# V in one piece, turned blocks in one piece, and four PSUM banks around layer 1's attention

## The chip, the cores and the metric

The kernel runs on one core of a Trainium2 chip. The metric is the device time of one execution in microseconds (us), here the median of several runs. Profiles are of one execution each. A core has TensorE (PE; its weight loads are PEld), VectorE (DVE), ScalarE (ACT), GpSimd (POOL), SyncE (SP, which here issues nearly all DMAs), and 16 DMA engines.

## What is computed

A two-layer backbone over 1024 latent tokens and 256 context tokens, width 1024, all in fp32. Layer 0 mixes with pooling and differential attention, layer 1 with multi-head latent attention; each layer ends with a SwiGLU. The change lies in layer 1's mixer:

```python
    def keys_values(a):
        b, n, _ = a.shape
        ckv = a @ w_dkv
        c_kv = rmsnorm(ckv[..., :MLA_KV_RANK], kv_lat_g)
        k_rope = ckv[..., MLA_KV_RANK:]
        kvh = (c_kv @ w_ukv).reshape(b, n, MLA_HEADS, MLA_NOPE + MLA_V)
        k = jnp.concatenate([kvh[..., :MLA_NOPE],
                             jnp.broadcast_to(k_rope[:, :, None, :], (b, n, MLA_HEADS, MLA_ROPE))], axis=-1)
        return rmsnorm(k, k_g), kvh[..., MLA_NOPE:]
...
    o_l = sweep_query_blocks(lambda qi, kk, vv: attn_core(qi, kk, vv, scale), q_l, k_all, v_all)
    out_l = o_l.reshape(b, n, MLA_HEADS * MLA_V) @ w_out
```

There are 16 heads, with 96 values per query and key (64 and 32 rotated) and 64 per V. The last layer needs latent queries only, so scores are 1024 queries by 1280 keys per head.

## The kernel before

All products are made from a high and a low part: fp32 operands are split into `hi` (rounded) and `lo` (the rest), and a product is three matmuls, hi x hi, hi x lo and lo x hi (`products`, L163). BANK is 512 fp32 columns, a PSUM bank; T is 1280 tokens in TT = 10 tiles of 128, LAT 1024 in QT = 8 tiles.

`heads1` (L656) goes through the 10 token tiles. For a tile, PE projects the queries (3 banks, L163 with `h1_wqh`; tiles 0 to 7 only), the keys (2 banks) and V in two halves of 512 columns (banks 5 and 2). DVE and ACT norm q and k. Between these projections PE turns blocks: turned block n takes two heads and 256 tokens by four transposes (L858) into a PSUM bank, ACT takes the high part out with its gain (`high`, L893), DVE the low part (`low`, L965), and SP stores both to DRAM (`store_turn`, L743). There are 72 such blocks, eight a tile, 20 slots behind the tile's own work, so that blocks 44 to 71 come in tiles 8 and 9 and after them. Block n uses one of two banks (TB + n % 2), so PE waits for `low` of block n - 2; the high and low parts lie in a ring of OUTS = 4 buffers each, so ACT waits for the stores of block n - 4. V goes the same way without a turn: `value_high` on ACT (L926), `value_low` on DVE (L1017), and two stores a half (L750).

In DRAM, q and k lie as one row of all tokens for each head, part (high or low) and value index: (32, 96, 1024) and (32, 96, 1280). A store of a block writes 192 pieces of 1 KB, a load of a head's k reads 96 pieces of 5 KB and of q 96 of 4 KB. V lies as two tensors, high and low.

`attention1` (L1066) then goes through the 16 heads; before it there is a barrier of all engines. Per head SP loads q high, k high, q low, k low (L1116, L1118) and then V high and V low (L1123, pieces of 256 B) into one of two buffers by the head's parity. The loads of head h wait until the scores of head h - 2 are done (`st`), V's also for the last product with V of that head (`pv`). PE first makes 20 units of high x high scores (`aux`, L1154 and L1159, two banks XB) whose maxima DVE takes (`read_aux`, L1228, L1230), then the negative maximum (L1234) is turned into a row of q (L1150, L1223). For head 0 all this is ahead of the loop; for head h + 1 it is spread over key tiles 1 to 8 of head h. In the loop, per key tile, PE makes scores of the next tile (six matmuls L163), ACT takes two exponentials a half (L1296, L1297), POOL their difference (L1323), and PE multiplies with V (L1184 to L1186). At the start DVE prepares constant rows (L1268 to L1275), for which PE waits (`rows`).

Each engine works strictly in the order of its own program; waits are on semaphores.

## Time and profile before

| | us |
|---|---|
| median of 3 runs | 3428.92 |
| lowest and highest | 3427.8, 3430.4 |
| the profiled execution's own time | 3422.42 |
| its span | 3420.6 |
| PE busy | 3168.6 (93%) |
| DVE, ACT, POOL busy | 1839.0, 973.2, 1507.9 |

The span is the time from the first to the last instruction. Times in the rows count from its start. `heads1` runs from about 1785 to 1982, `attention1` from there to about 2578. An engine's busy share over the whole says little about either; windows, waits and the timeline do. A wait is put down to the last releaser that the profile shows.

### The profile page before, as it was taken

How to read it: one execution, taken by the hardware profiler on the slowest of the kernel's cores; microseconds unless marked ns; L12 is line 12 of the kernel's file. 1: busy time of each engine (PE TensorE's matmuls, PEld its weight loads, DVE VectorE, ACT ScalarE, POOL GpSimd, SP SyncE). 2: the span in 40 equal slices, each digit the busy share in tenths (PEclk: the TensorE clock that was granted, in tenths of full speed). 3: DMA queues.
4: the chain of work that ended last, by engine and by line, in shares of the span. 5: the costliest groups of instructions: out<-in, count | busy, mean ns of one | idle time of the engine just before them, and what ended most of it. 6: DMA issues, size and time to landing. Idle time of an engine off the chain costs nothing. (4 is left out here: it accounts for less than half of the span.)

```text
span 3420.6 us, 42918 instructions
## 1 busy us (share of the span) xinstructions
PE 3168.6 (93%) x15030; PEld 2599.5 (76%) x15030; DVE 1839.0 (54%) x2477; ACT 973.2 (28%) x1698; POOL 1507.9 (44%) x1157
## 2 busy tenths in 40 slices
PE   7997987799999999999889879999996999999999
PEld 6775775588888888888677657777775788888887
DVE  5584876655444444444526757777666433333333
ACT  4322664131000000000424536666661300000000
POOL 3683543543322332222522237777787533332332
PEclk9998998899999999999989979999998999999999
DMA  6466221412222222222214862332314211111111
GB/s 225 130 198 174 55 55 64 156 56 73 69 65 64 61 61 63 65 67 62 80 48 157 263 174 63 69 73 58 84 29 154 62 50 44 53 44 43 55 49 62
DMA packets 160193, 297.26 MB, mean 87 GB/s; under 512 B 53345, under 2 KB 98145, under 8 KB 159969
## 3 DMA queue, kind: packets, MB, share of 16 engines
q1 hardware_dynamic: 148576, 254.08, 25.2%
q10 hardware_dynamic: 11520, 41.95, 4.3%
q8 instruction: 54, 0.88, 0.1%
q14 instruction: 43, 0.34, 0.0%
HBM read 233.06 MB, written 62.91 MB: 87 GB/s over the span
## 5 line engine op out<-in xcount | busy, mean ns | idle before, releaser
L127 POOL TENSOR_TENSOR small<-ident 128x1 f32<-128x1 f32 x170 | 53.8, 316 | 1165.9 <-PE ps L163 663.5
L163 PE MATMUL ps<-hidden,whi 128*128 128x512 f32 (+1 forms) x1760 | 500.7, 370 | 8.6 <-POOL wlo L138 5.1
L1323 POOL TENSOR_TENSOR a_pl<-a_p,a_ph 128x512 fp32r<-128x512 f32 x320 | 430.4, 1367 | 173.6 <-ACT a_p L1297 173.2
L1989 DVE SCALAR_TENSOR_TENSOR residual<-ps,mod,residual 128x512 f32<-128x512 f32 (+1 forms) x440 | 302.6, 696 | 376.1 <-PE ps L163 376.0
L138 POOL TENSOR_TENSOR wlo<-raw,whi 128x1024 fp32r<-128x1024 f32 x170 | 440.7, 2592 | 14.2
L163 PE MATMUL ps<-mixed_hi,whi 128*128 128x512 f32 (+1 forms) x1200 | 426.5, 355 | 14.3 <-POOL wlo L138 10.4
L163 PE MATMUL ps<-mixed_lo,whi 128*128 128x512 f32 (+1 forms) x1200 | 425.3, 354 | 0.0
L163 PE MATMUL ps<-mixed_hi,wlo 128*128 128x512 f32 (+1 forms) x1200 | 424.9, 354 | 0.0
L163 PEld LDWEIGHTS ps<-hidden,whi 128*128 128x128 f32 x1760 | 320.3, 189 | 65.4 <-POOL wlo L138 5.2
L1800 ACT ACTIVATE hidden<-gated 128x512 fp32r<-128x512 f32 (+1 forms) x110 | 64.9, 590 | 999.9 <-DVE gated L1978 999.8
L1978 DVE TENSOR_TENSOR gated<-gated,ps 128x512 f32<-128x512 f32 (+1 forms) x110 | 69.8, 635 | 511.6 <-PE ps L163 495.4
L163 PE MATMUL ps<-o_hi,whi 128*128 128x512 f32 x800 | 314.1, 393 | 24.6 <-POOL wlo L138 20.6
L163 PE MATMUL ps<-hidden,wlo 128*128 128x512 f32 (+1 forms) x880 | 324.6, 369 | 0.0
L163 PE MATMUL ps<-o_hi,wlo 128*128 128x512 f32 x800 | 312.8, 391 | 0.0
L163 PE MATMUL ps<-o_lo,whi 128*128 128x512 f32 x800 | 312.7, 391 | 0.0
L163 PE MATMUL ps<-a_q,a_k 97*128 97x512 f32 x960 | 270.1, 397 | 0.8 <-DVE a_q L1223 0.8
L163 PEld LDWEIGHTS ps<-mixed_hi,whi 128*128 128x128 f32 x1200 | 227.3, 189 | 48.4 <-POOL wlo L138 11.0
L163 PEld LDWEIGHTS ps<-mixed_lo,whi 128*128 128x128 f32 x1200 | 227.4, 190 | 31.4
L163 PEld LDWEIGHTS ps<-mixed_hi,wlo 128*128 128x128 f32 x1200 | 227.1, 189 | 31.7
L1296 ACT ACTIVATE a_ph<-ps 128x512 fp32r<-128x512 f32 x320 | 192.4, 601 | 182.0 <-PE ps L163 180.8
L1228 DVE TENSOR_REDUCE a_top<-ps 128x1 f32<-128x512 f32 x256 | 176.2, 691 | 75.5 <-PE ps L1154 70.5
L163 PEld LDWEIGHTS ps<-a_q,a_k 97*128 97x128 f32 x960 | 180.5, 190 | 38.9 <-DVE a_q L1223 1.0
(293 smaller groups left out, 6079.3 us busy)
## 6 DMA issues: line engine op xcount, KB each, us to landing
raw<-in_w_ffn SPq DMA_DIRECT2D x132, 512.0 KB, 3.6
l_vraw<-in_mod_t ACTq DMA_DIRECT2D x56, 512.0 KB, 3.7
raw<-in_w_out SPq DMA_DIRECT2D x32, 512.0 KB, 3.7
a_k<-scratch_k SPq DMA_DIRECT2D x32, 480.0 KB, 6.8
f_vraw<-in_mod_t ACTq DMA_DIRECT2D x24, 512.0 KB, 4.2
a_q<-scratch_q SPq DMA_DIRECT2D x32, 384.0 KB, 5.7
a_k<-scratch_k SPq DMA_DIRECT2D x32, 320.0 KB, 7.3
a_v<-scratch_v SPq DMA_DIRECT2D x32, 320.0 KB, 5.1
```

Of the source, the lines that this page charges most:

```text
L127: e.nc.gpsimd.tensor_tensor(e.spare[:, 0:1], e.ident[:, 0:1], e.ident[:, 0:1], ALU.mult)
L138: nc.gpsimd.tensor_tensor(e.wlo[:, s, 0:n], e.raw[:, s, 0:n], e.whi[:, s, 0:n].bitcast(F32), ALU.subtract).then_inc(e.split_done, 1)
L163: last = nc.tensor.matmul(out, a, b, start=at == 0, stop=at == n - 1)
L1228: nc.vector.tensor_reduce(top[:, q:q + 1, c], e.ps[:, bank:bank + BANK], AX.X, ALU.max).then_inc(s["auxr"], 1)
L1296: nc.scalar.activation(ph[:, kk % 2, c], b, ACT.Exp).then_inc(s["exp"], 1)
L1323: nc.gpsimd.tensor_tensor(pl[:, kk % 2, c], p[:, kk % 2, c], ph[:, kk % 2, c].bitcast(F32), ALU.subtract).then_inc(s["pl"], 1)
L1800: nc.scalar.activation(hh[:, y, a:a + w], hm[:, a:a + w], ACT.Copy).then_inc(s["hi"], 1)
L1978: nc.vector.tensor_tensor(hm[:, a:a + w], sg[:, a:a + w], e.ps[:, 3 * BANK + a:3 * BANK + a + w], ALU.mult).then_inc(s["prod"], 1)
L1989: last = nc.vector.scalar_tensor_tensor(h[:, m, a:a + w], e.ps[:, o:o + w], e.mod[:, g, c:c + 1], h[:, m, a:a + w], ALU.mult, ALU.add)
```

## The change

- V is stored whole, one store a half, from `value_high` alone; the DVE step `value_low` leaves `heads1`. In `attention1` V is loaded whole (one load a head) into a new buffer, ACT copies it into the high part at key tile 4 of the head before (`value_high`), and DVE subtracts at key tile 5 (`value_low`). V's load now waits only for that subtraction two heads earlier.
- In DRAM q and k lie as (8 pairs of heads, 2 parts, 96, groups of 256 tokens, 2 heads, 256). A store of a block is 96 pieces of 2 KB; a load of q is 96 x 4 pieces of 1 KB, of k 96 x 5.
- At the start of `attention1` SP loads high q and high k of head 0 on a semaphore of their own and waits for them before it issues the rest.
- The first 20 maxima and the two rows after them go round four banks (XB and OB) instead of two; the turned blocks from n = 44 on go round four (TB and the query banks, free by then).

```diff
@@ heads1
+        vw = sb("h1_v", [128, 2, BANK], F32)
...
+        WIDE = 8 * QT - 20
+        def turn_bank(n):
+            return TB + n % 2 * BANK if n < WIDE else (TB, TB + BANK, QB, QB + BANK)[(n - WIDE) % 4]
+        def turn_before(n):
+            return max((m for m in range(n) if turn_bank(m) == turn_bank(n)), default=None)
...
                     for x, buf in enumerate((oh, ol)):
-                        to = dst[4 * u8:4 * u8 + 4, :, 256 * g:256 * g + 256].rearrange("(h x) d t -> x d h t", x=2)
-                        sp.dma_start(to[x, :, :, :], buf[:, n % OUTS, :].rearrange("p (h t) -> p h t", h=2).bitcast(F32))\
+                        sp.dma_start(dst[u8, x, :, g, :, :].rearrange("d h t -> d (h t)"), buf[:, n % OUTS, :].bitcast(F32))\
...
                 def store_v(t, half):
-                    sp.wait_ge(s["vlo"], n + 1)
-                    for x, buf in enumerate((vh, vl)):
-                        sp.dma_start(S["v1"][x, t, :, half * BANK:(half + 1) * BANK], buf[:, n % 2, :].bitcast(F32))\
-                          .then_inc(vstored[n % 2], 16)
+                    sp.wait_ge(s["vcopy"], n + 1)
+                    sp.dma_start(S["v1"][t, :, half * BANK:(half + 1) * BANK], vw[:, n % 2, :]).then_inc(vstored[n % 2], 16)
...
-                    if n >= 2:
-                        pe.wait_ge(s["lo"], n - 1)
-                    bank = TB + (n % 2) * BANK
+                    if turn_before(n) is not None:
+                        pe.wait_ge(s["lo"], turn_before(n) + 1)
+                    if n >= WIDE:
+                        pe.wait_ge(s["qs"], 2 * QT)
+                    bank = turn_bank(n)
...
-                def value_low(t, n):
-                    dve.wait_ge(s["vhi"], 2 * t + n + 1)
-                    nc.vector.scalar_tensor_tensor(vl[:, n, :], e.ps[:, VBANK[n]:VBANK[n] + BANK], rc[:, t:t + 1], vh[:, n, :].bitcast(F32),
-                                                   ALU.mult, ALU.subtract).then_inc(s["vlo"], 1)
@@ attention1, SP
-                def load(h, par, first):
+                def load(pair, par, first):
+                    h = pair * 2 + par
                     if not first:
                         sp.wait_ge(s["st"], h * 2 * KS - 2 * KS)
                     for x in range(2):
+                        at = s["early"] if first and par == 0 and x == 0 else s[f"qk{par}"]
...
+                        if at is s["early"]:
+                            sp.wait_ge(at, 32)
                     if not first:
-                        sp.wait_ge(s["pv"], h * KS - KS + 2)
-                    for x, at in ((0, 0), (1, 2 * VD1)):
-                        sp.dma_start(vs[:, par, :, at:at + VD1].bitcast(F32),
-                                     S["v1"][x, :, :, bass.ds(h * VD1, VD1)].rearrange("t p v -> p t v"))\
-                          .then_inc(s[f"v{par}"], 16)
+                        sp.wait_ge(s["vlo"], h)
+                    sp.dma_start(vw[:, par, :, :], S["v1"][:, :, bass.ds(h * VD1, VD1)].rearrange("t p v -> p t v"))\
+                      .then_inc(s[f"v{par}"], 16)
@@ attention1, PE
-                def aux(g, par, u):
+                def aux(g, par, u, first=False):
                     bank = XB + (u % 2) * BANK
+                    if first:
+                        bank = (XB, XB + BANK, OB, OB + BANK)[u % 4]
                     if u == 0:
-                        pe.wait_ge(s[f"qk{par}"], (g - par) * 32 + 64)
+                        if first:
+                            pe.wait_ge(s["early"], 32)
+                        else:
+                            pe.wait_ge(s[f"qk{par}"], (g - par) * 32 + 64)
...
-                    pe.wait_ge(s["auxr"], g * AUX + u + 1)
+                    if not first:
+                        pe.wait_ge(s["auxr"], g * AUX + u + 1)
+                    elif u >= 4:
+                        pe.wait_ge(s["auxr"], u - 1)
@@ attention1, DVE
+                    if kk == 5 and more:
+                        value_low(h + 1, 1 - par)
+                def value_low(g, par):
+                    dve.wait_ge(s["vhi"], g + 1)
+                    nc.vector.tensor_tensor(vs[:, par, :, 2 * VD1:3 * VD1], vw[:, par, :, :], vs[:, par, :, 0:VD1].bitcast(F32),
+                                            ALU.subtract).then_inc(s["vlo"], 1)
@@ attention1, ACT
+                    if kk == 4 and more:
+                        value_high(h + 1, 1 - par)
+                def value_high(g, par):
+                    act.wait_ge(s[f"v{par}"], (g - par) * 8 + 16)
+                    nc.scalar.activation(vs[:, par, :, 0:VD1], vw[:, par, :, :], ACT.Copy).then_inc(s["vhi"], 1)
@@ scratch
-            ("q1", (HEADS1 * 2, QK1, LAT), F32), ("k1", (HEADS1 * 2, QK1, T), F32),
-            ("v1", (2, TT, 128, HEADS1 * VD1), F32), ("h", (KT, 128, LAT), F32))}
+            ("q1", (HEADS1 // 2, 2, QK1, LAT // 256, 2, 256), F32), ("k1", (HEADS1 // 2, 2, QK1, T // 256, 2, 256), F32),
+            ("v1", (TT, 128, HEADS1 * VD1), F32), ("h", (KT, 128, LAT), F32))}
```

SP's order at the entry of attention stands like this before (`a_q`, `a_k`, `a_v` are head 0's and then head 1's buffers):

```order
L1116 DMA a_q<-scratch_q 96x1024
L1118 DMA a_k<-scratch_k 96x1280
L1116 DMA a_q<-scratch_q 96x1024
L1118 DMA a_k<-scratch_k 96x1280
L1123 DMA a_v<-scratch_v 128x10x64 x2
```

and like this in the changed kernel, where `a_vw` is the new buffer for whole V and `f_mfull3` is the number that the new semaphore got:

```order
L1119 DMA a_q<-scratch_q 96x4x256
L1121 DMA a_k<-scratch_k 96x5x256
L1119 DMA a_q<-scratch_q 96x4x256 [waits f_mfull3]
L1121 DMA a_k<-scratch_k 96x5x256
L1127 DMA a_vw<-scratch_v 128x10x64
```

The wait now stands between the high and the low parts, the pieces are 256 columns, and one load of V is gone.

PE's first products of head 0 (units 0 to 15 are 512 columns wide), before; `f_stored0` is what DVE's reading of a maximum raises:

```order
L1154 MATMUL ps<-a_k,a_q 128x512 [waits f_stored0,f_mfull4,f_vfull0]
L1154 MATMUL ps<-a_k,a_q 128x512 [waits f_stored0] x15
```

and changed:

```order
L1165 MATMUL ps<-a_k,a_q 128x512 [waits f_mfull3,f_vfull0]
L1165 MATMUL ps<-a_k,a_q 128x512 x3
L1165 MATMUL ps<-a_k,a_q 128x512 [waits f_stored0] x12
```

The first product waits for the new semaphore and, as before, for the constant rows (`f_vfull0`); three more follow with no wait for DVE.

DVE in the last token tile of `heads1`, before (`h_vl` is V's low part, `h_ol` a turned block's, L982 the sum of squares of k):

```order
L1017 SCALAR_TENSOR_TENSOR h_vl<-ps,heads_spare,h_vh 128x512 [waits f_xa7]
L965 SCALAR_TENSOR_TENSOR h_ol<-ps,h_kgain,h_oh 96x512 [waits f_xa5]
L982 TENSOR_REDUCE heads_spare<-heads_spare 128x16 [waits f_rot,f_root]
L965 SCALAR_TENSOR_TENSOR h_ol<-ps,h_kgain,h_oh 96x512 [waits f_xa5]
L1017 SCALAR_TENSOR_TENSOR h_vl<-ps,heads_spare,h_vh 128x512 [waits f_xa7]
L965 SCALAR_TENSOR_TENSOR h_ol<-ps,h_kgain,h_oh 96x512 [waits f_xa5] x2
```

and changed:

```order
L974 SCALAR_TENSOR_TENSOR h_ol<-ps,h_kgain,h_oh 96x512 [waits f_xa5] x2
L991 TENSOR_REDUCE heads_spare<-heads_spare 128x16 [waits f_rot,f_root]
L974 SCALAR_TENSOR_TENSOR h_ol<-ps,h_kgain,h_oh 96x512 [waits f_xa5] x3
```

Both subtractions for V are gone; the order of the rest is the same.

## Rows read from the trace of the kernel before

**Rows 1.** The page, the chain that ended last: shares of the span by engine.

```profile
PE 23%; DVE 1%; issue 0%; POOL 0%; ACT 0%; DMA 0%; DVEq 0%; SPq 0%; POOLq 0%
```

**Rows 2.** Windows: us, busy PE, PEld, DVE, ACT, POOL, granted clock, DMA share, GB/s.

```profile
1925.00:1958.00 33.00, 26.20 (x127) 18.93 (x127) 23.52 (x35) 18.38 (x30) 6.02 (x6) 0.90 0.90 280
1958.00:1982.00 24.00, 10.52 (x48) 6.42 (x48) 11.62 (x17) 8.34 (x13) 1.05 (x1) 0.64 0.89 272
```

**Rows 3.** Waits of PE, 1850 to 1925: us in total, times, longest us.

```profile
PE ps L858 <- DVE h_ol L965: 5.7, 4, 1.4
```

**Rows 4.** Waits of PE and of ACT, 1925 to 1958.

```profile
PE ps L858 <- DVE h_ol L965: 5.8, 8, 1.4
...
ACT h_oh L893 <- DMA scratch_q<-h_ol: 4.8, 4, 2.5
```

**Rows 5.** Waits of PE and of ACT, 1958 to 1982.

```profile
PE ps L858 <- DVE h_ol L965: 8.7, 10, 2.0
...
ACT h_oh L893 <- DMA scratch_k<-h_ol: 6.4, 6, 2.0
```

**Rows 6.** Timeline at the entry: start us, us, what, [idle before <- releaser].

```profile
1982.13 0.34 SPq L1116 DMA_DIRECT2D a_q<-scratch_q  x1
...
1989.11 0.49 DVE L1275 CAST a_v<-sel 128x640 fp32r<-128x640 f32 x1
...
1991.27 1.19 PE L1154 MATMUL ps<-a_k,a_q 96*128 96x512 f32 x2 [15.17 <-DMA a_k<-scratch_k]
...
1992.08 1.29 DVE L1228 TENSOR_REDUCE a_top<-ps 128x1 f32<-128x512 f32 x2 [2.48 <-PE ps L1154]
...
1993.65 1.29 DVE L1228 TENSOR_REDUCE a_top<-ps 128x1 f32<-128x512 f32 x2 [0.29 <-PE ps L1154]
...
2007.60 0.18 DVE L1234 TENSOR_REDUCE a_negmax<-a_top 128x8 fp32r<-128x24 f32 x1
...
2010.59 5.38 PE L163 MATMUL ps<-a_q,a_k 97*128 97x512 f32 x12 [0.79 <-DVE a_q L1223]
```

**Rows 7.** Windows, the loop.

```profile
2070.00:2500.00 430.00, 419.92 (x1882) 322.63 (x1880) 309.37 (x408) 279.20 (x519) 332.78 (x246) 1.00 0.31 69
```

**Rows 8.** Waits of PE, 2016 to 2500.

```profile
PE ps L1154 <- DMA a_k<-scratch_k: 3.0, 4, 1.3
```

**Rows 9.** Groups, 1785 to 1982: busy us, mean ns of one | idle before.

```profile
L1017 DVE SCALAR_TENSOR_TENSOR h_vl<-ps,heads_spare,h_vh 128x512 fp32r<-128x512 f32 x20 | 14.8, 740 | 4.2 <-ACT h_vh L926 4.1
...
L926 ACT ACTIVATE h_vh<-ps,heads_spare 128x512 fp32r<-128x512 f32 x20 | 13.6, 681 | 15.0 <-PE ps L163 15.0
```

**Rows 10.** Windows: q and k of head 0; the residual in 4 KB pieces.

```profile
1984.00:1986.00 2.00, 0.00 (x0) 0.00 (x0) 1.97 (x4) 0.00 (x0) 0.00 (x0) 0.50 1.07 305
...
2008.00:2010.00 2.00, 1.80 (x8) 1.61 (x8) 0.86 (x2) 0.00 (x0) 0.00 (x0) 0.50 1.02 408
```

**Rows 11.** Windows: q and k in the loop (4, 5 KB); V (256 B).

```profile
2048.00:2049.00 1.00, 1.00 (x6) 0.70 (x4) 0.00 (x0) 1.00 (x2) 1.00 (x2) 1.00 1.01 254
...
2052.00:2053.00 1.00, 0.34 (x2) 0.30 (x2) 0.00 (x0) 0.61 (x2) 0.80 (x2) 1.00 1.37 219
```

**Rows 12.** Timeline, the last turned blocks.

```profile
1973.49 0.68 ACT L893 ACTIVATE h_oh<-ps,h_kgain 96x512 fp32r<-96x512 f32 x1 [1.00 <-PE ps L858]
...
1975.17 0.75 DVE L965 SCALAR_TENSOR_TENSOR h_ol<-ps,h_kgain,h_oh 96x512 fp32r<-96x512 f32 x1 [0.22 <-ACT h_oh L893]
...
1976.14 0.68 ACT L893 ACTIVATE h_oh<-ps,h_kgain 96x512 fp32r<-96x512 f32 x1 [1.00 <-PE ps L858]
```

**Rows 13.** The page, DMA issues: count, KB each, median us from issue to landing.

```profile
scratch_k<-h_oh SPq DMA_DIRECT2D x40, 192.0 KB, 2.8
```

**Rows 14.** Timeline in the loop: ScalarE ahead of a key tile's first exponential.

```profile
2063.46 0.60 ACT L1296 ACTIVATE a_ph<-ps 128x512 fp32r<-128x512 f32 x1 [1.42 <-PE ps L163]
```

**Rows 15.** Timeline, a head without a wait: its load's issue, its first product.

```profile
2114.08 0.34 SPq L1116 DMA_DIRECT2D a_q<-scratch_q  x1
...
2123.08 0.44 PE L1154 MATMUL ps<-a_k,a_q 96*128 96x512 f32 x1
```

More of the change, by code:

```diff
@@ L760, in _ @@
                 for x in range(2):
-                    sp.wait_ge(vstored[x], 32 * TT)
+                    sp.wait_ge(vstored[x], 16 * TT)
             @block.gpsimd
@@ L834, in value @@
                     if n == 0 and t:
-                        pe.wait_ge(s["vlo"], 2 * t - 1)
+                        pe.wait_ge(s["vcopy"], 2 * t - 1)
                     if n == 1:
@@ L924, in value_high @@
                     if t:
-                        act.wait_ge(vstored[n], 32 * t)
-                    nc.scalar.activation(vh[:, n, :], e.ps[:, VBANK[n]:VBANK[n] + BANK], ACT.Copy, scale=rc[:, t:t + 1]).then_inc(s["vhi"], 1)
+                        act.wait_ge(vstored[n], 16 * t)
+                    nc.scalar.activation(vw[:, n, :], e.ps[:, VBANK[n]:VBANK[n] + BANK], ACT.Copy, scale=rc[:, t:t + 1]).then_inc(s["vcopy"], 1)
                 for x in range(7):
@@ L1060, in _ @@
                     low(t, 6)
-                    if t < TT:
-                        value_low(t, 1)
                     low(t, 7)
@@ L1074, in attention1 @@
         vs = sb("a1_v", [128, 2, TT, 3 * VD1], F32R)
+        vw = sb("a1_vw", [128, 2, TT, VD1], F32)
         p = sb("a1_p", [128, 2, LAT], F32)
@@ L1079, in attention1 @@
         ident = sb("a1_ident", [128, 128], F32R)
-        s = {x: sem("a1_" + x) for x in ("qk0", "qk1", "v0", "v1", "rows", "aux", "auxr", "neg", "st", "exp", "pl",
-                                         "pv", "raw", "rec", "whole", "ohi", "out", "x")}
+        s = {x: sem("a1_" + x) for x in ("early", "qk0", "qk1", "v0", "v1", "rows", "aux", "auxr", "neg", "st", "exp", "pl",
+                                         "pv", "raw", "rec", "whole", "ohi", "out", "x", "vhi", "vlo")}
         OB, XB = 4 * BANK, 6 * BANK
@@ L1115, in load @@
                     for x in range(2):
-                        sp.dma_start(qs[0:QK1, par, x, :].bitcast(F32), S["q1"][bass.ds(h * 2 + x, 1), :, :]
-                                     .rearrange("o p t -> p (o t)")).then_inc(s[f"qk{par}"], 16)
-                        sp.dma_start(ks[0:QK1, par, x, :].bitcast(F32), S["k1"][bass.ds(h * 2 + x, 1), :, :]
-                                     .rearrange("o p t -> p (o t)")).then_inc(s[f"qk{par}"], 16)
-                    if not first:
-                        sp.wait_ge(s["pv"], h * KS - KS + 2)
-                    for x, at in ((0, 0), (1, 2 * VD1)):
-                        sp.dma_start(vs[:, par, :, at:at + VD1].bitcast(F32),
-                                     S["v1"][x, :, :, bass.ds(h * VD1, VD1)].rearrange("t p v -> p t v"))\
-                          .then_inc(s[f"v{par}"], 16)
+                        at = s["early"] if first and par == 0 and x == 0 else s[f"qk{par}"]
+                        sp.dma_start(qs[0:QK1, par, x, :].rearrange("d (g t) -> d g t", t=256).bitcast(F32),
+                                     S["q1"][bass.ds(pair, 1), x, :, :, par, :].rearrange("o d g t -> d (o g) t")).then_inc(at, 16)
+                        sp.dma_start(ks[0:QK1, par, x, :].rearrange("d (g t) -> d g t", t=256).bitcast(F32),
+                                     S["k1"][bass.ds(pair, 1), x, :, :, par, :].rearrange("o d g t -> d (o g) t")).then_inc(at, 16)
+                        if at is s["early"]:
+                            sp.wait_ge(at, 32)
+                    if not first:
+                        sp.wait_ge(s["vlo"], h)
+                    sp.dma_start(vw[:, par, :, :], S["v1"][:, :, bass.ds(h * VD1, VD1)].rearrange("t p v -> p t v"))\
+                      .then_inc(s[f"v{par}"], 16)
                 load(0, 0, True)
-                load(1, 1, True)
+                load(0, 1, True)
                 for k in range(KT):
@@ L1131, in _ @@
                 with each(sp, HEADS1 // 2 - 1) as i:
-                    load(i * 2 + 2, 0, False)
-                    load(i * 2 + 3, 1, False)
+                    load(i + 1, 0, False)
+                    load(i + 1, 1, False)
                 sp.wait_ge(s["x"], 16 * KT)
@@ L1177, in value @@
                     if kk == 0 and x == 0:
-                        pe.wait_ge(s[f"v{par}"], (h - par) * 16 + 32)
+                        pe.wait_ge(s["vlo"], h + 2)
                         pe.wait_ge(s["raw"], h + 1)
@@ L1206, in _ @@
                 for u in range(AUX):
-                    aux(0, 0, u)
+                    aux(0, 0, u, True)
+                pe.wait_ge(s["qk0"], 64)
                 for x in range(2):
@@ L1217, in _, with read_aux @@
             def _(dve):
-                def read_aux(g, par, u):
-                    bank = XB + (u % 2) * BANK
+                def read_aux(g, par, u, first=False):
+                    bank = (XB, XB + BANK, OB, OB + BANK)[u % 4] if first else XB + (u % 2) * BANK
                     dve.wait_ge(s["aux"], g * AUX + u + 1)
@@ L1277, in _ @@
                 for u in range(AUX):
-                    read_aux(0, 0, u)
+                    read_aux(0, 0, u, True)
+                value_low(0, 0)
                 walk(dve, step)
@@ L1310, in high @@
                     nc.scalar.activation(place(oh, par, tile), whole[64 * par:64 * par + 64, :], ACT.Copy).then_inc(s["ohi"], 1)
+                act.wait_ge(s["rows"], 10)
+                value_high(0, 0)
                 walk(act, step)
```

17 lines of the change are left out of this document (7 added, 10 removed).

## Prediction

> **What bounds the kernel now.** I read the chain that ended last first. It only says that TensorE is the engine that counts [rows 1], and it stops before the layer-1 loop, so the place of the change has to be read from windows. The change touches three stretches: the end of the head projection (`heads1`, up to 1982 us), the entry of attention (1982 to 2011) and the attention loop (2011 to about 2570).
>
> In the windows of the projection the reader should look at two columns, PE busy and the DMA share. Between 1925 and 1958 PE is busy for 26.2 of 33 us with the DMA engines at 0.90; between 1958 and 1982 it is busy for 10.5 of 24 us, DMA still at 0.89 [rows 2]. Before 1925 TensorE is nearly full, and its only wait on what the change touches is 5.7 us in 75, for a bank that `low` has to free [rows 3]. Then two waits share the rest: PE waits for DVE (5.8 us, then 8.7), and ScalarE waits for stores to give back an output buffer (4.8 us, then 6.4) [rows 4, 5]. So the tail has two limits at nearly one height: the turned blocks go round two PSUM banks, and the stores fill the DMA engines.
>
> At the entry PE stands still from the end of the projection to 1991.27, waiting for the first heads' loads, and then works in pairs with DVE until 2007.60 [rows 6]. In the loop PE is busy for 419.9 of 430 us [rows 7], so whatever holds PE there costs its own length, and the only wait on a load is 3.0 us in 4 pieces [rows 8].
>
> The sum is made against the profiled span, 3420.6 us in a run of 3422.42. The median of the runs is 3428.92, 6.5 above that run; a difference in the span is carried over to the median as it is.
>
> **Turned blocks and V in the projection.** Each of the 20 halves of V loses a DVE subtraction of 0.740 us [rows 9] and one of its two stores. Up to 1925 I cost this at nothing: PE is the bound, and the `low` for which it waits [rows 3] stands ahead of the removed subtraction in DVE's order. If PE were not the cover, it would be worth at most 20 x 0.74 = 14.8 us.
>
> For the DMA side I need the price of a piece. On one of 16 engines a piece takes size x 16 x share / rate. The 4 KB pieces of the residual give 4096 x 16 x 1.02 / 408 = 164 ns [rows 10], the 256 B pieces of V 256 x 16 x 1.37 / 219 = 25.6 ns [rows 11]: a fixed 16.4 ns and 36 ns per KB. That predicts 53.3 ns for 1 KB, and the store stretch gives 1024 x 16 x 0.89 / 272 = 53.6 [rows 2]. A turned block is stored as high and low of 96 rows, 6 rows an engine: 2 x 12 x 53.3 = 1.28 us now, 2 x 6 x 90 = 1.08 us when each row is one piece of 2 KB. A V store of 128 rows of 2 KB costs 8 x 90 = 0.72 us and is saved twice per token tile.
>
> From 1925 on there are 28 turned blocks (the ones that get four banks) and at least 4 halves of V. Were DMA the only limit, the saving would be 28 x 0.20 + 4 x 0.72 = 8.5 us; this is the upper bound. But the ring of four output buffers stays: ScalarE 0.68, DVE 0.75 [rows 12], the issue and about 2.8 us to landing [rows 13] make some 5.2 us for 4 blocks, 1.3 us a block. The last blocks now run at (1976.14 - 1973.49) / 2 = 1.33 us [rows 12]. So four banks take away PE's wait for DVE and bring almost nothing for the last 12 blocks (about 1 us, from landings that come sooner), since the ring is next. In token tiles 8 and 9, where projections and blocks alternate, the waits of 5.8 and 4.8 us overlap; I take 4 us of the 33. Together 5.0 us, bounds 2.5 (the V stores of two tiles alone, 4 x 0.72, a little hidden) and 8.5.
>
> **The entry.** Only high q and high k of head 0 are loaded first, 0.88 MB instead of 1.77. At 305 GB/s [rows 10] that is 2.9 us, with 2 us to land (9.0 less 7.0 us, below) and the issue about 5.5, so it lands near 1987.6. But PE also waits for DVE's preparation of the constant rows, which this change keeps; it ends at 1989.11 + 0.49 = 1989.60 [rows 6]. PE starts at about 1989.7 instead of 1991.27: 1.55 us, not the 3.7 that the loads alone would give.
>
> The 20 first maxima take from 1991.27 to 2007.60, and a pair repeats every 1993.65 - 1992.08 = 1.57 us though DVE needs 1.29 for it; the second of a pair starts 0.60 after the first [rows 6]. With four banks DVE sets the pace. At 0.60 each: 0.81 us to the first, 19 x 0.60 + 0.69, so 12.9 us instead of 16.3, 3.4 us gained; if a wait stays between any two, 0.69 each, 14.6 us, 1.7 gained. PE can follow even at the 1.2 GHz level that these rows show (granted clock 0.50, [rows 10]): 12 products in 5.38 us are 0.45 each [rows 6]. I take 3.3. What was late next, low q, low k and V, has from 1987.6 to about 2004; 1.2 MB need 5 us. The conversion of V for head 0 lies in the 4 us between the first scores and the first product with V. Entry: 4.8 us, bounds 3.2 and 5.0.
>
> **The loop, work added.** Each head adds one ScalarE copy of 640 columns and one DVE subtraction. From 0.68 and 0.74 us for 512 columns [rows 9] they are at most 0.85 and 0.93. ScalarE idles 1.42 us per key tile before its first exponential [rows 14], so the copy fits. DVE is busy for 309 of 430 us [rows 7]; after key tile 5 it falls behind by less than the two-bank distance of the maxima and catches up in tile 7, which has one maximum fewer. I cost both at nothing; without that cover, 15 x 0.93 = 14 us. SP no longer waits for the product with V before it loads V; that lets V's load queue sooner, behind q and k of the same head.
>
> **The loop, loads in pieces.** This is the open term. Each q row now comes in 4 pieces of 1 KB and each k row in 5, where it was one of 4 or 5 KB. PE starts a head's maxima 9.00 us after the load was issued in a head that shows no wait (2114.08 to 2123.08) [rows 15]. 1.77 MB at 254 GB/s [rows 11] are 7.0 us, with 2 for latency 9.0: there is no slack at all. An engine has 6 rows of each of 4 tensors, so by the piece prices above these loads should take 12 x (4 + 5) x 53.3 ns = 5.8 us in pieces of 1 KB; they take 7.0 now, although a 5 KB piece should need only 201 ns (at 254 GB/s and share 1.01 it needs 326, [rows 11]). Something slows the large pieces that did not slow 1 KB stores. If small pieces escape it, the 3.0 us of waits go. If they only keep today's time, nothing changes. If both costs add, the fixed 16.4 ns comes on top for 3 + 4 extra pieces: 12 x 7 x 16.4 ns = 1.38 us a load, 14 x 1.38 = 19.3 us. I take 2.0 gained, since the 1 KB rows lie nearest, and keep -19.3 and +3.0 as ends.
>
> The Trainium skill, page DMA: Bandwidth & Descriptors, section Why small descriptors are slow (HBM only), speaks against this part: a fixed overhead of some 3 cycles per packet beside one cycle per 32 bytes. By its figures five pieces of 1 KB take 5 x 35 against 163 cycles, 7% more, an estimate of 0.5 us a load and 7 us over 14 heads, which would bring the sum to about 3426. The trace agrees that small pieces cost more per byte [rows 10, 11], but shows this load slower than that rule in its large pieces already, so I don't follow it.
>
> **Sum.** 5.0 + 4.8 + 2.0 = 11.8 us, 3428.9 - 11.8 = 3417.1.
>
> **Rivals.**
> (A) *Pieces add to the load.* 9.8 us gained in projection and entry, 19.3 lost on PE in the loop: 3438. For it: no slack [rows 15], and V's 256 B pieces do pay [rows 11]. Against it: 1 KB stores ran at the full price of the fit. It decides from 9.8 / 14 = 0.7 us more per load; from 1.2 us the kernel is measurably slower.
> (B) *Half of that shows*, 0.7 us a load, 9.7 us: gain and loss cancel, 3429. The skill's rule, above, ends beside it.
> (C) *DMA is the real limit of the tail and stores of 2 KB free it*: 8.5 in the projection, 5.0 at the entry, 3.0 in the loop and a clock that rises earlier at the entry (up to 1.5): 18 us, 3411.
> (D) *The banks do nothing*, since the ring and DVE's order hold the pace: 2.5 + 3.2 + 0: 3423. That is the change not doing what it says.
>
> **Chances.** Forecast 0.55, C 0.15, D 0.08, B 0.14, A 0.08. The range runs from C's side, 3409, to the near side of B, 3427. A measurement of this kernel can tell about 0.2% (6.9 us) from no change. Faster by more: the forecast, C and half of D, with a little taken off for the forecast's weak end: 0.74. Within: 0.18. Slower: A, 0.08.
>
> **What would show it.** In the new profile: PE's first product of head 0 right behind DVE's last preparation; a pitch of 0.60 to 0.69 us of the first 20 maxima; blocks at the end of the projection at about 1.2 to 1.3 us with PE's wait for `low` gone and ScalarE's wait for stores left; first maxima of a head 9.0 us or less after their load's issue, with less than 3.0 us of PE waits on a1_k. Wrong if those waits come to 10 us or more (A, B), if the projection up to 1925 changes (it should not), or if PE waits for the maxima around key tile 6.

## The result and the profile of the changed kernel

| | before | changed |
|---|---|---|
| runs of one comparison, median (lowest to highest), us | 3428.55 (3427.8 to 3430.4) | 3458.53 (3452.05 to 3460.39) |
| ratio, 95% interval | | 1.0087 (1.0074 to 1.0100) |
| profiled run, its span, us | 3422.42, 3420.6 | 3460.39, 3458.4 |

The changed kernel is slower by 30 us; a gain of 11.8 us was forecast. The profiled runs stand 37.8 us apart, because the one of before is 6 us under its median and the one of the changed kernel 2 us above. The readings below are of these two.

At the entry, answering [rows 6] (start us, us, what, idle before and its releaser):

```profile
1980.00 1.76 DVE L1288 MEMSET a_p<- 1x2048 f32 x1 [4.43 <-PEq L731]
1980.12 0.68 SPq L1119 DMA_DIRECT2D a_q<-scratch_q  x1
...
1986.40 0.56 SPq L1119 DMA_DIRECT2D a_q<-scratch_q  x1
...
1987.53 8.95 PE L1165 MATMUL ps<-a_k,a_q 96*128 96x512 f32 x16 [16.18 <-DVE a_v L1295]
...
1988.36 9.66 DVE L1240 TENSOR_REDUCE a_top<-ps 128x1 f32<-128x512 f32 x16 [0.89 <-PE ps L1165]
...
2000.44 0.18 DVE L1246 TENSOR_REDUCE a_negmax<-a_top 128x8 fp32r<-128x24 f32 x1
...
2003.48 0.76 PE L163 MATMUL ps<-a_q,a_k 97*128 97x512 f32 x1 [0.84 <-issue]
```

PE now starts right behind DVE's preparation, and DVE reads 16 maxima in 9.66 us, 0.60 each. From the first instruction of the entry to the first scores it takes 2003.48 - 1980.00 = 23.5 us; before it was 28.5.

In the loop, PE's waits from 2025 to 2550 (us in total, times, longest), answering [rows 8]:

```profile
PE ps L1165 <- DMA a_k<-scratch_k: 24.0, 14, 2.8
PE ps L1170 <- DVE a_top L1240: 9.7, 13, 0.8
```

The first line stood at 3.0 us in 4 pieces before; now every head waits. The second wait did not exist before. For the first, a load's issue and the head's first maximum, answering [rows 15]:

```profile
2115.12 0.60 SPq L1119 DMA_DIRECT2D a_q<-scratch_q  x1
...
2117.40 0.56 SPq L1121 DMA_DIRECT2D a_k<-scratch_k  x1
2118.15 0.48 SPq L1127 DMA_DIRECT2D a_vw<-scratch_v  x1
...
2125.64 0.49 PE L1165 MATMUL ps<-a_k,a_q 96*128 96x512 f32 x1 [1.38 <-DMA a_k<-scratch_k]
```

That is 10.52 us instead of 9.00. Over the 14 heads loaded in the loop it is 10.82 us on average (10.46 to 11.38) against 9.22 (8.98 to 10.05): 14 x 1.60 = 22.4 us. The seven microseconds that begin one after the issue show the rate; before, then changed (granted clock, DMA share and GB/s are the last three numbers):

```profile
2115.08:2122.08 7.00, 6.33 (x26) 4.23 (x25) 2.40 (x3) 5.75 (x11) 5.91 (x5) 1.00 1.01 262
```

```profile
2116.12:2123.12 7.00, 6.34 (x26) 4.24 (x25) 2.41 (x3) 5.78 (x12) 5.92 (x5) 1.00 0.95 233
```

For the second wait, the changed kernel's DVE, GpSimd (POOL) and PE around V's new subtraction, and the group of its 16:

```profile
2103.84 2.54 POOL L1353 TENSOR_TENSOR a_pl<-a_p,a_ph 128x512 fp32r<-128x512 f32 x2 [0.92 <-ACT a_p L1318]
...
2105.41 1.65 DVE L1266 TENSOR_TENSOR a_v<-a_vw,a_v 128x640 fp32r<-128x640 f32 x1
...
2107.10 0.95 DVE L1274 RECIPROCAL a_recip<-a_raw 64x128 f32<-64x128 f32 x1
...
2108.65 0.50 PE L1170 MATMUL ps<-a_k,a_q 96*128 96x256 f32 x2 [0.74 <-DVE a_top L1240]
```

```profile
L1266 DVE TENSOR_TENSOR a_v<-a_vw,a_v x16: 825/1651/1674, 2003.4 to 2560.0; 128x640 fp32r<-128x640 f32 x16
```

It takes 0.825 us at the entry, where GpSimd rests, and 1.65 in the loop. It begins 1.57 us into GpSimd's pair. The 0.83 us by which it is too long, counted from its start, run to 2106.24, close to the end of that pair at 2106.38. The stretch from a head's first maximum to the next load's issue is 26.7 us instead of 25.65 in the heads with an undisturbed clock: 13 x 1.06 = 13.8 us, of which 9.7 are PE's wait above.

The rest is TensorE's clock. After the longest wait (windows: us, busy PE, granted clock, DMA share, GB/s):

```profile
2047.49 0.79 PE L1165 MATMUL ps<-a_k,a_q 96*128 96x512 f32 x1 [2.83 <-DMA a_k<-scratch_k]
```

```profile
2044.00:2048.00 4.00, 1.17 (x4) 0.86 1.00 169
2048.00:2052.00 4.00, 4.00 (x11) 0.50 0.02 4
2052.00:2056.00 4.00, 4.00 (x16) 0.79 0.00 0
```

0.50 is the 1.2 GHz level: 11 products in 4 us, where a row at 1.00 of the same place has 19 (e10, below). That head's stretch takes 29.54 us, three later ones, behind waits of 1.73, 1.96 and 2.20 us, 28.26 to 28.29; together 2.8 + 3 x 1.57 = 7.5 us over 26.7.

So the loop loses 22.4 + 13.8 + 7.5 us, and projection (-4.3) and entry (-5.0) give back 9.3. With the projection's start 2.1 us later and some 1.3 us in the first and last heads that makes the 37.8.

### The profile page after: what moved, and what is told of

Read it like the earlier page. It is cut to its first block and busy times, and to the rows that moved or that the text cites. A ratio compares the mean times of both kernels' runs of the same rounds, so it can differ in the third digit from the quotient of the medians.

```text
span 3458.4 us, 42876 instructions
## 1 busy us (share of the span) xinstructions
PE 3178.6 (92%) x15030; PEld 2602.8 (75%) x15030; DVE 1850.0 (53%) x2473; ACT 984.1 (28%) x1714; POOL 1510.4 (44%) x1157
## 5 line engine op out<-in xcount | busy, mean ns | idle before, releaser
L138 POOL TENSOR_TENSOR wlo<-raw,whi 128x1024 fp32r<-128x1024 f32 x170 | 440.7, 2592 | 14.2
```

Of the source, the lines that this page charges most:

```text
L138: nc.gpsimd.tensor_tensor(e.wlo[:, s, 0:n], e.raw[:, s, 0:n], e.whi[:, s, 0:n].bitcast(F32), ALU.subtract).then_inc(e.split_done, 1)
```

## The experiments

A table of all kernels first. "Projection" is from ScalarE's first weight split (1787.94 before) to DVE's first operation of the entry (1982.13), "entry" from there to the first scores; "load" is the mean over 14 heads from a load's issue to the first maximum, "head" the mean over 13 from there to the next issue. The ratio is to the kernel before, run beside each. All columns behind the ratio come from one profile of each kernel. How far one profile can be trusted shows in e1 and e12, whose attention is the same code: their "load" differs by 0.36 us, which is 5 us over 14 loads.

| kernel | us | ratio (95%) | projection | entry | load | head |
|---|---|---|---|---|---|---|
| before | 3428.6 | | 194.2 | 28.5 | 9.22 | 25.65 |
| changed | 3458.5 | 1.0087 (1.0074 to 1.0100) | 189.9 | 23.5 | 10.82 | 27.29 |
| e1 old rows | 3433.6 | 1.0016 (1.0007 to 1.0026) | 188.5 | 23.5 | 9.57 | 26.70 |
| e2 new rows only | 3462.6 | 1.0093 (1.0072 to 1.0114) | 194.1 | 30.3 | 10.77 | 26.66 |
| e3 late V | 3439.3 | 1.0034 (1.0019 to 1.0048) | 190.3 | 23.5 | 10.74 | 26.01 |
| e6 old rows, late V | 3421.6 | 0.9983 (0.9974 to 0.9993) | 189.2 | 23.5 | 9.64 | 25.63 |
| e8 old rows, V split | 3423.4 | 0.9984 (0.9974 to 0.9993) | 195.2 | 23.5 | 9.52 | 25.81 |
| e10 wait for high parts | 3425.3 | 0.9991 (0.9982 to 1.0001) | 189.6 | 23.4 | 8.96 | 26.60 |
| e11 the same, late V | 3417.2 | 0.9969 (0.9956 to 0.9981) | 188.4 | 23.4 | 9.48 | 25.60 |
| e12 old rows, two banks | 3435.6 | 1.0022 (1.0013 to 1.0032) | 188.3 | 23.5 | 9.21 | 26.67 |
| e13 e10, one input | 3422.8 | 0.9976 (0.9967 to 0.9986) | 188.2 | 23.4 | 8.95 | 26.28 |
| e14 e11, behind GpSimd | 3413.6 | 0.9956 (0.9939 to 0.9973) | 190.5 | 23.4 | 9.12 | 25.60 |
| e15 e10, V split | 3416.0 | 0.9963 (0.9949 to 0.9977) | 194.3 | 23.4 | 8.91 | 25.59 |
| e16 e6, behind GpSimd | 3419.5 | 0.9972 (0.9960 to 0.9983) | 193.7 | 23.5 | 9.41 | 25.66 |
| f1 e1, two issues a load | 3444.9 | 1.0059 (1.0042 to 1.0076) | 193.3 | 23.5 | 10.07 | 26.70 |
| f2 q alone in pieces | 3444.4 | 1.0055 (1.0038 to 1.0071) | 190.0 | 23.5 | 10.18 | 26.82 |

**Are the pieces the cause of the late loads? e1 and e2.** e1 is the changed kernel with the old rows of q and k in DRAM, e2 the kernel before with the new ones alone.

```diff
 e1, store and load (e2 does the reverse to the kernel before)
-    sp.dma_start(dst[u8, x, :, g, :, :].rearrange("d h t -> d (h t)"), buf[:, n % OUTS, :].bitcast(F32))
+    to = dst[4 * u8:4 * u8 + 4, :, 256 * g:256 * g + 256].rearrange("(h x) d t -> x d h t", x=2)
+    sp.dma_start(to[x, :, :, :], buf[:, n % OUTS, :].rearrange("p (h t) -> p h t", h=2).bitcast(F32))
...
-    S["q1"][bass.ds(pair, 1), x, :, :, par, :].rearrange("o d g t -> d (o g) t")
+    S["q1"][bass.ds(h * 2 + x, 1), :, :].rearrange("o p t -> p (o t)")
```

> The changed kernel with q and k in DRAM as they were: blocks stored in 192 pieces of 1 KB, a head's q and k loaded in 96 rows of 4 and 5 KB. All else of the change stays. Theory P (the 1 KB pieces make the loads late): first maximum of a head 9.0 to 9.5 us after its load's issue instead of 10.8, PE's waits on a_k back from 24.0 to about 3 us, no stretch of the loop at a granted clock under 0.95, the wait for DVE's maxima stays near 9.7; total about 3435 us. Theory V (V's load, which no longer waits for the product with V, crowds q and k): 10.5 us or more to the first maximum, waits above 20 us, total 3455 us.

> The kernel before with the new DRAM layout of q and k alone (blocks stored in 96 pieces of 2 KB, q and k loaded in pieces of 1 KB). Theory P: first maximum 10.5 to 11 us after the load's issue, PE's waits on a_k 20 us or more, clock dips in the loop, total 3450 to 3458 us. Theory V: 9.0 to 9.5 us and 3425 to 3429 us.

PE's waits from 2025 to 2550 in e2:

```profile
PE ps L1154 <- DMA a_k<-scratch_k: 23.9, 14, 3.9
```

The new rows alone bring the whole wait, and 34 us, into the kernel before, whose V still waits its turn on SyncE. That is 5 us more than theory P gave: the entry, which waits for all four loads there, is 1.8 us longer too, and the clock fell in eight of 13 heads, 1.6 us each. The old rows take the wait out of the changed kernel (6.3 us, 10 times, left) and with it the drops of the clock. V's load, which the changed kernel issues 0.75 us after the last k, e2 3.5 us and the kernel before 4.2 us after it, is not the cause.

**Does the subtraction in the loop cost? e3 and e6.** V's copy and subtraction moved behind the maxima, with the new rows (e3) and with the old (e6).

```diff
-                    if kk == 4 and more:    (ACT)   if kk == 5 and more:    (DVE)
+                    if kk == 8 and more:            if kk == 9 and more:
```

> The changed kernel with V's copy at key tile 8 and its subtraction at key tile 9 instead of 4 and 5. Theory S (the subtraction, 1.65 us beside a busy POOL, delays the maxima of tile 6): PE's wait for a_top goes from 9.7 us to under 1, a head's stretch from its first maximum to the next load's issue from 26.71 to 25.7 us, total 3444 us. Rival (it costs wherever it stands, as POOL or DVE loses the time anyway): PE's wait for a_pl grows from 8.6 to 15 us or more and the total stays above 3452 us.

> Both: q and k in DRAM as before the change, and V's copy and subtraction at key tiles 8 and 9. If P and S hold and are all of the loss, what is left is the gain of the projection and the entry: 3419 to 3423 us, faster than the kernel before by about 7 us. If the subtraction costs anywhere: 3430 to 3435 us.

PE's waits from 2025 to 2550 in e6:

```profile
PE ps L1196 <- POOL a_pl L1354: 18.1, 29, 0.9
PE ps L1166 <- DMA a_k<-scratch_k: 1.5, 2, 1.1
```

The wait for DVE is gone and "head" is back at 25.6, but the wait for GpSimd grew from about 9 to 18 us (16.2 in e3). So the rival of e3 was right about that wait and wrong about the time: e3 is 19 us faster than the changed kernel, 5 more than forecast. There the longer wait for GpSimd lies ahead of the wait for the load, which is 15.5 us instead of 24.0. e6 gains 0.33% (11 us) on e1, not the 13.8 us in full: part of the cost moved to another engine.

**Which part brings what in front of the loop? e8 and e12.** e8 is e1 with V split in the projection as before, so only the early high parts and both sets of banks are left. e12 is e1 with two banks for the turned blocks to the end.

```diff
 e12
-        WIDE = 8 * QT - 20
+        WIDE = TURNS
 e8: value_low and the two stores and loads of V as in the kernel before, no copy or subtraction in the loop
```

> The changed kernel without two of its parts: q and k stored and loaded in the old rows, and V split in the projection and stored and loaded as two parts, as before. What is left is the early high parts, the four banks for the first maxima and the four banks for the last turned blocks. Theory S (the V work placed in the loop costs some 1.05 us a head): against the kernel with the old rows alone (3433.6 us) the 14 heads give back 14.7 us, so 3419 us if the four banks for the turned blocks brought the 4.8 us of the projection, and 3424 us if V's missing low parts brought it. Rival R (the time between a head's first maximum and the next load is longer for another reason, the waits or the order on SyncE): 3430 us or more, and that stretch stays at 26.7 us instead of 25.7.

> The changed kernel with the old rows, and without the four banks for the last turned blocks (two banks to the end, as before); V is stored whole and the entry is as changed. If the four banks bring the projection's 4.8 us, it is 3438.4 us against 3433.6 us of the kernel with the old rows alone, and the entry begins about 5 us later. If V's missing low parts bring them, 3433.6 us and no change of where the entry begins. I lean to a division: 3 us to the banks, 2 us to V, 3436.6 us.

Both answer the same: the projection takes 188.3 us with V whole and two banks (e12), 195.2 with V split and four banks (e8). The four banks bring nothing there. PE's wait for the bank doubles in e12, from 5.5 in e1 to 11.5 us between 1925 and 1982, yet the stretch is no longer: with four banks TensorE waits less for a bank and more for the normed k (5.2 us against 1.8). With four banks the clock also falls in the ninth stretch between two tiles' squares of k, in twelve of the thirteen kernels that have them (13.7 to 14.4 us at 0.88); the three with two banks stay at 1.00 (13.1 to 13.6 us). The medians of e12 and e1 can't tell that (2 us apart), and that e12 came out near my divided 3436.6 is luck; the stages do. Of the gain between V split and V whole, 2.7 us lie in one token tile, and they are the clock's; where e1 and e12 are ahead of the changed kernel, 1.5 us are the clock's in the first tile (13.9 us against 15.4). Windows of the one tile, from its squares of k on ScalarE to those of the next, in before, e8, e12 and e16 (columns as in [rows 2]):

```profile
1923.66:1939.47 15.81, 12.24 (x51) 8.76 (x51) 11.18 (x16) 7.73 (x13) 4.97 (x5) 0.78 0.83 258
```

```profile
1923.33:1939.20 15.87, 11.95 (x51) 8.97 (x51) 11.16 (x16) 7.61 (x13) 5.00 (x5) 0.78 0.84 257
```

```profile
1929.91:1943.03 13.12, 9.31 (x51) 6.85 (x51) 9.92 (x14) 7.59 (x14) 5.00 (x5) 1.00 0.81 248
```

```profile
1928.25:1943.91 15.66, 11.99 (x51) 9.08 (x51) 9.93 (x14) 7.70 (x14) 4.98 (x5) 0.78 0.74 227
```

The four kernels with V split (before, e2, e8, e15) all take 15.8 to 15.9 us for this tile. Of the twelve with V whole nine take 13.1 and f2 13.8; e16 and f1 take 15.7 and 15.6, and their projections 193.7 and 193.3. All sixteen have the same wait of PE at the start of this tile, 1.39 to 1.43 us, so the wait alone does not decide. In each profile one earlier tile also takes 19.0 us instead of 17.4, at a granted clock of 0.91. Where that is the fourth stretch between two squares (nine kernels, the four with V split among them), the clock falls again in this tile in seven, and in three of the five with V whole; where it comes later (seven kernels, all with V whole), in none. So the 2.7 us go with the place of the earlier falls as much as with V, and that V earned them is not shown. The last stretch, from the last squares of k to the entry, is the steadier part: 29.0 and 29.3 us with V split and old rows (before, e8), 29.1 and 28.1 with V split and new rows (e2, e15), 27.4 to 27.7 with V whole and k in old rows (e1, e6, e12, e16, f1, f2), 26.5 to 27.2 with V whole and new rows. With V whole, the stores of 2 KB are worth the last 0.8 us.

**Must the pieces cost? e10 and e11.** The first maximum needs only the high parts. In e10 it waits for these alone in every head, in e11 V is late as well.

```diff
-                        at = s["early"] if first and par == 0 and x == 0 else s[f"qk{par}"]
+                        at = s["early"] if first and par == 0 and x == 0 else s[f"qk{par}" if x else f"hp{par}"]
 aux, u == 0
-                            pe.wait_ge(s[f"qk{par}"], (g - par) * 32 + 64)
+                            pe.wait_ge(s[f"hp{par}"], (g - par) * 16 + 32)
 scores, kk == 0
+                        pe.wait_ge(s[f"qk{par}"], (h - par) * 16 + 32)
```

> The changed kernel, but in every head the first maximum waits for the two high-part loads alone, and the scores wait for the two low parts. Theory P (the pieces of 1 KB make the four loads of a head land late, and that is all they do): the high parts land in time, the waits on a_k (24.0 us) and the drops of the clock behind them (7.5 us) go, so 3427 to 3434 us, 9.2 us from issue to first maximum. Rival Q (slower transfers also hold back something later, V's load or the low parts at the scores): waits return on the scores or on V, and the time stays above 3440 us.

> The changed kernel with both repairs: the first maximum waits for the high parts alone in every head, and V's copy and subtraction stand behind the last row of maxima (steps 8 and 9 of a head instead of 4 and 5). If the two causes are all there is, it does as well with the pieces of 1 KB as the kernel with the old rows and the late subtraction (3421.6 us): 3418 to 3423 us. If the pieces cost in another way too, 3427 us or more.

PE's waits from 2025 to 2550 in e10, and its windows at the place where the changed kernel's clock fell:

```profile
PE ps L1170 <- DVE a_top L1240: 10.4, 14, 0.7
PE ps L1196 <- POOL a_pl L1353: 9.4, 28, 0.4
```

```profile
2044.00:2048.00 4.00, 4.00 (x19) 1.00 0.97 184
2048.00:2052.00 4.00, 4.00 (x19) 1.00 0.00 0
```

No wait for a load is left, the clock stays at the 2.4 GHz level, and no wait comes back on the scores: 33 us less than the changed kernel, and 2 us below the range of theory P. e11 is 1 us below its range. The loads are as late as ever: the low parts land 10.4 us after the first issue in e10, 10.7 in the changed kernel. But the high parts are there after 6.6 us, and "load" is 8.96. With these waits no wait of PE is left that the pieces could cause; a kernel with these waits and the old rows was not run.

**What holds the subtraction? e13 and e14.** In e13 (e10 otherwise) V's low part is made from one tile, V times zero, so the low part of V is left out of the values, not of the work. In e14 (e11 otherwise) the subtraction waits for GpSimd's second subtraction of its step.

```diff
 e13
-   nc.vector.tensor_tensor(vs[:, par, :, 2 * VD1:3 * VD1], vw[:, par, :, :], vs[:, par, :, 0:VD1].bitcast(F32), ALU.subtract)
+   nc.vector.tensor_scalar(vs[:, par, :, 2 * VD1:3 * VD1], vw[:, par, :, :], 0.0, None, ALU.mult)
 e14, kk == 9
+                        dve.wait_ge(s["pl"], (h * KS + kk) * 2 + 2)
                         value_low(h + 1, 1 - par)
```

> The kernel in which the first maxima wait for the high parts alone (3425.3 us), with V's low part made by an operation of one input at the same place (V times zero; the low parts of V are therefore zero, and that part of the product is left out in value, not in time). Theory L (DVE's subtraction reads two tiles of SBUF and can't run beside GpSimd's subtraction, which is why it takes 1.65 us instead of 0.82): the operation with one input takes under 0.9 us beside GpSimd, PE's wait on a_top (10.4 us) goes, the stretch from a head's first maximum to the next load falls from 26.6 to 25.7 us, and the time is 3425.3 - 13 = 3412 us. Rival C (any work at this place of DVE's order makes the maxima late): the stretch stays above 26.1 us and the time above 3419 us.

> The kernel with both repairs (3417.2 us), and DVE's subtraction of V now waits for GpSimd's second subtraction of its step (step 9). GpSimd stands idle for 0.94 us between its pairs and the subtraction alone takes 0.82. Theory L: it takes 0.82 to 0.9 us in every head, GpSimd is not held, PE's waits on a_pl fall from 17.9 back to about 9.4 us, the time from issue to first maximum falls from 9.6 to 9.1 us, and the kernel is at 3417.2 - 7.7 = 3409.5 us (3407 to 3413). Rival W (the wait only moves the delay, since DVE's next head or PE's product with V then comes late): 3416 us or more.

The operation of e13, and around that of e14 and of e11 (GpSimd and DVE):

```profile
L1266 DVE TENSOR_SCALAR a_v<-a_vw x16: 496/1317/1345, 2006.6 to 2523.6; 128x640 fp32r<-128x640 f32 x16
```

```profile
2141.43 1.89 DVE L1267 TENSOR_TENSOR a_v<-a_vw,a_v 128x640 fp32r<-128x640 f32 x1 [2.43 <-POOL a_pl L1354]
```

```profile
2108.34 4.34 POOL L1353 TENSOR_TENSOR a_pl<-a_p,a_ph 128x512 fp32r<-128x512 f32 x3 [1.86 <-ACT a_p L1318]
2108.51 1.80 DVE L1266 TENSOR_TENSOR a_v<-a_vw,a_v 128x640 fp32r<-128x640 f32 x1
...
2111.49 0.49 PE L1196 MATMUL ps<-a_ph,a_v 128*128 128x512 f32 x1 [0.84 <-POOL a_pl L1353]
```

My theory, that it is the two inputs that can't run beside GpSimd, fell with e13: the operation with one input is held as long, 1.317 - 0.496 = 0.82 us, like 1.651 - 0.825 = 0.83. What e13 gained (0.15% by the ratios, 5 us; 2.5 us by the medians) is the 0.33 us by which it is shorter itself; PE's wait per head fell from 0.74 to 0.41. Not every operation is held: the maxima, which read PSUM, take 0.69 us beside GpSimd and without, and the reciprocal of 64 x 128 in SBUF, with one input, 0.94 against 0.89. In e11 both engines pay: three of GpSimd's subtractions take 4.34 us, not 3.87, and PE waits for one. The Trainium skill, page SBUF — State Buffer, section SBUF: two separate sides, states that DVE and GpSimd share one pair of ports as an exclusive lock, taken by DVE for operations with two SBUF inputs or in a mode that uses two ports; whichever engine comes second stands still until the other's instruction ends. The traces agree, with 0.82 us in each form, and in e11 it is GpSimd that is held. In which mode e13's operation ran, no run shows.

For e14 an operation of 0.9 us was forecast; it takes 1.89 in every head of the loop, because GpSimd is behind at a head's end and starts its next pair at once. But nobody waits for DVE there, and PE's wait for GpSimd is back at 9.9 us. So part of the gain came (0.13%, 4 of 7.7 us in the medians, just outside the forecast's 3407 to 3413, and the two intervals overlap), by another way than I said.

**What is V whole worth? e15, and the same wait with old rows, e16.** e15 is e10 with V split, stored and loaded as before; e16 is e6 with e14's line.

> The changed kernel with the high parts waited for alone in every head, and V split, stored and loaded as before. Against the same kernel with V whole (3425.3 us) it loses what V whole gains in the projection (5.9 us by the stages of the two kernels with V split and V whole) and gives back what its subtraction costs in the loop (13.0 us): 3418 us. If V whole gains nothing in the projection: 3412 us. If the subtraction isn't what costs: 3431 us.

> The changed kernel with the old rows of q and k, and V's subtraction in step 9 behind GpSimd's second subtraction of that step. Against the same kernel without that wait (3421.6 us): 7.7 us less by theory L, 3414 us; no change by rival W. Against the kernel with the new rows and the waits for high parts alone it shows what the pieces are worth once the waits are right: its a_k waits (1.5 us) and the stores of 1 KB at the end of the projection should put it 1 to 4 us above that one.

e15 is 9 us below e10, where 7 were expected: V whole, as the change places it, costs more than it brings. In its best place (e14) it is level with V split, 3413.6 against 3416.0, intervals overlapping. e16 missed by 5 us: it gained 2 us on e6, not 7.7. Its wait for GpSimd fell as in e14 (18.1 to 9.6 us), but with the old waits the loads take over: PE waits for them six times, 2.7 us, and "load" falls by 0.23 us only, against 0.36 from e11 to e14. In its profile, the slowest of seven runs, the clock in the one tile shown above costs another 2.5 us; whether it fell in the others is not on record.

**Issue or transfer? f1 and f2.** In f1 (e1 otherwise) each load is issued as two of 48 rows; in f2 only q lies in pieces.

```diff
 f1
-    sp.dma_start(qs[0:QK1, par, x, :].bitcast(F32), S["q1"][bass.ds(h * 2 + x, 1), :, :] ...
+    for r in (slice(0, 48), slice(48, 96)):
+        sp.dma_start(to[r, par, x, :].bitcast(F32), S[src][bass.ds(h * 2 + x, 1), r, :] ...
```

> The changed kernel with the old rows of q and k (whole rows of 4 and 5 KB), but each of a head's four loads is issued as two DMAs of 48 rows each. The pieces stay large, and only SyncE's time per tensor grows: two issues of about 0.33 us instead of one, near the 0.57 us that a load in pieces of 1 KB takes. Theory I (the loads in pieces are late because SyncE issues them more slowly): issue to first maximum goes from the 9.57 us of the kernel with the old rows to about 10.8 us, PE waits 20 us or more on a_k, and the time is 3451 us or more. Theory T (they are late because the transfers themselves are slower, 233 GB/s against 262): 9.3 to 9.9 us, and 3432 to 3437 us.

> The changed kernel with q in pieces of 1 KB and k in its old rows, so a half dose: 3 extra pieces of the 7, and 2 of the 4 long issues. If each extra piece costs the same, issue to first maximum is 9.57 + 3/7 of 1.25 = 10.1 us and the time some 3444 us. If k, whose loads are the later ones, carries the cost alone, 9.6 us and 3434 us; if q does, 10.8 us and 3455 us.

f1 issues a tensor in 0.81 us, longer than the pieces take (0.57), and "load" grows by 0.50 us: not the 1.25 of theory I, and more than the 0.3 that theory T allows. Its time, 3444.9 us, lies between the two as well. But f1 does not change the issue alone. The loads' queue in the loop (2025 to 2550; packets, MB, share of 16 engines' time) in e1, f1 and the changed kernel:

```profile
q1 hardware_dynamic: 24416, 29.36, 23.8%
```

```profile
q1 hardware_dynamic: 25312, 29.37, 26.0%
```

```profile
q1 hardware_dynamic: 43232, 29.36, 26.1%
```

The same bytes keep the engines busy as long in f1, in large pieces but in DMAs of 3 rows an engine, as in the changed kernel. So f1's loss is one of transfer, and it says nothing of the issue. The packets' own times do: their first one starts 0.95 to 0.99 us after the issue in every kernel with q in old rows, f1 too, and 1.38 to 1.40 where q lies in pieces. From e1 to the changed kernel that is 0.43 us later, and from the first packet to the end of the last it takes 8.39 us instead of 7.61 (means of 14 loads). The two together are 1.21 of the 1.25 us: about a third is the later start, two thirds the transfer. Against e12, whose loads take 7.21 us, the transfer's part would be 1.18, so only the start is known to a tenth.

f2, with 3 of 7 extra pieces, has 0.61 of the 1.25, where 0.54 was expected, and its time is the forecast 3444. That looks like a cost by the number of pieces, but its first packet starts as late as in the changed kernel, at 1.39, so 0.43 of its 0.61 us is that start, which q's first load brings alone. The agreement is in part luck.

## Why the prediction was wrong

**Projection, forecast -5.0, measured -4.3.** The number held, its working did not, so that is luck. It gave 4 us to the four banks in the token tiles 8 and 9. e12 and e8 show that the banks bring nothing. Of what the changed kernel gained, 2.3 us lie behind the last squares of k (some 1.5 by V's missing stores and operations, 0.8 by the stores of 2 KB), where about 1 was forecast, and 2.7 us in the tile after the queries, where PE's clock no longer fell, a term that the forecast did not have; 0.8 us were lost elsewhere. "PE's wait for `low` gone" was wrong too: 5.9 of 13.4 us stayed (the 5.8 and 8.7 of [rows 4, 5] count one wait across 1958 twice). That the ring of output buffers is next was right: ScalarE's waits for stores between 1925 and 1982 are 14.2 us, 12.7 before.

**Entry, forecast -4.8, measured -5.0.** Each step as told: PE starts behind the preparation, 0.60 us a maximum.

**Added work in the loop, forecast 0, measured +13.8.** The failed step is "I cost both at nothing": the subtraction was priced at 0.93 us at most, from an operation of 512 columns in the projection, where GpSimd does little. Beside GpSimd's pair it is 1.65, more than the banks of the maxima can cover, and PE waits 0.74. That 13.8 lies so near the 14 us that the prediction named for "without that cover" is chance: it took 15 x 0.93. The forecast counted DVE's busy time and the order on it, and not what runs on the other engine at that moment. The trace of before could have warned: there GpSimd's subtraction takes 1.29 us in the middle, but up to 2.28. The copy on ScalarE is free as told, 0.76 us.

**Loads in pieces, forecast -2.0, measured +22.4 us and 7.5 of clock.** The failed step is the value taken of the open term. Both ends were there, and the loss of 1.38 us a load, rival A, was worked out from rows; measured were 1.6. I weighed it at 0.08, since 1 KB stores stood nearest, though the term itself says "no slack at all" [rows 15] and V's small pieces did pay [rows 11]. The price of 53.3 ns for a piece of 1 KB, from stores, did not hold for loads: by the changed kernel's window above a piece takes 1024 x 16 x 0.95 / 233 = 67 ns, so 108 of them 7.2 us and not 5.8. And the pieces start later, 0.43 us, a term that the sum did not have. The Trainium skill, page DMA: Bandwidth & Descriptors, section Why small descriptors are slow (HBM only), pointed the right way with its fixed cost per packet; its 0.5 us a load, an estimate by its figures, is a third of what was measured. That waits on PE of 1.7 to 2.8 us also slow the work after them was in no rival. The chance of "slower" was far too small for a sum whose largest term was the open one.

## What to carry over

Where a load has no slack, its transfer's shape is on the critical path of every iteration: price pieces by loads that are waited for, and wait for the part that the first consumer needs (e10: 33 us of 3458) before arguing about the shape. Before placing a DVE operation on SBUF tiles in a loop, look at what GpSimd runs at that moment and take the duration beside it; if it can't be kept apart, put it where nobody waits for DVE (e14, 0.44% faster than before, the best of all). When a stage gains what was forecast, take its parts out one by one before crediting any: here the four banks for the turned blocks got the credit and brought nothing. And compare two profiles of the same code before reading a part of a microsecond out of one: here 0.36 us a load is between two of them.

## What the runs showed of the hardware

- A DVE operation over 128 x 640 in SBUF is held beside GpSimd's subtraction, with one input (0.50 to 1.32 us, e13) as with two (0.83 to 1.65, changed kernel); maxima read from PSUM are not (0.69), nor is the reciprocal of 64 x 128 (0.89 to 0.94).
- A wait of 2.83 us on PE was followed by some 6 us at or partly at the 1.2 GHz level and cost 2.8 us more; waits of 1.73, 1.96 and 2.20 us cost 1.6 us each in the changed kernel, others of 1.79 and 2.13 nothing. In e2 one of 3.90 us cost 1.6 as well, in f1 one of 2.41 nothing: the length of the wait alone does not tell the cost.
- SyncE issues a load of 96 rows in 4 or 5 pieces each in 0.57 us, in whole rows in 0.33, and the first packet starts 1.39 us after the issue instead of 0.96.
- 1.77 MB in 1 KB pieces come 1.25 (against e1) to 1.6 us (against before) later than in pieces of 4 and 5 KB. A packet of 1 KB takes 69 ns in these loads, one of 5 KB 321 to 323 (means of the changed kernel, before and e1).
